# Feed-forward up projections: one 512-column matmul over both parts of the activations, and the closing steps moved to VectorE

## The reference, cut to what matters

```python
for i in range(4):
    ...
    h = modulate_2(rms_norm_2(x, norm_g[i, 2]), sh_f, sc_f)
    y = jnp.square(jax.nn.relu(h @ ffn_w1[i])) @ ffn_w2[i]
    x = x + g_f[:, None, :] * rms_norm_2(y, norm_g[i, 3])
```

## Time and profile before

| | us |
|---|---|
| median of 3 runs | 3532.57 |
| lowest and highest | 3532.52, 3533.49 |
| the profiled execution, its own time | 3530.79 |
| its span in the profile | 3528.8 |
| TensorE busy in the span | 2957.8 (84%) |
| VectorE busy | 1101.8 (31%) |
| ScalarE busy | 989.0 (28%) |

### The profile page before, as it was taken

The page is one execution under the profiler, slowest core; times in us unless marked ns, Lnnn a source line. Parts: engine busy times, 40 slices in busy tenths (PEclk is TensorE's granted clock), DMA queues, the critical chain, the costliest instruction groups (busy, mean ns, idle before and its releaser), DMA issues.

```text
span 3528.8 us, 40562 instructions
## 1 busy us (share of the span) xinstructions
PE 2957.8 (84%) x16176; PEld 1959.7 (56%) x16176; DVE 1101.8 (31%) x1997; ACT 989.0 (28%) x1818; POOL 55.1 (2%) x51
## 2 busy tenths in 40 slices
PE   5999787777789678787787997878998978988898
PEld 2343432222464342222356897666887867875797
DVE  1174200000131320000035444344436345433454
ACT  1211211110121210000034444334434444433443
POOL 0030000000000000000000000000000000000000
PEclk9999899999899789999988998769998999998899
DMA  9683089999512039999912664105664324751141
GB/s 402 258 352 160 25 361 428 428 428 428 230 72 76 0 123 428 429 428 428 428 51 96 252 276 189 48 21 212 268 262 152 144 96 176 293 204 72 49 180 70
DMA packets 59987, 796.13 MB, mean 226 GB/s; under 512 B 9114, under 2 KB 10029, under 8 KB 11501
## 3 DMA queue, kind: packets, MB, share of 16 engines
q1 hardware_dynamic: 54576, 788.03, 54.0%
q10 hardware_dynamic: 5309, 6.69, 0.6%
HBM read 793.64 MB, written 1.05 MB: 225 GB/s over the span
## 4 chain that ended last, share of the span: by engine, by line
PE 68%; DMA 18%; DVE 5%; ACT 5%; issue 2%; ACTq 1%; SPq 0%; DVEq 0%; POOL 0%; POOLq 0%
DMA ring<-in_t_up 15%; PE banks L1574 11%; PE banks L1564 10%; PE banks L733 8%; PE banks L872 8%; PE banks L1195 7%; PE banks L1069 4%; PE banks L639 3%; PE banks L854 2%; DMA ring<-in_t_down 2%; ACT arena L677 1%; PE banks L1169 1%; PE banks L1211 1%; PE banks L1226 1%; PE banks L1304 1%
## 5 line engine op out<-in xcount | busy, mean ns | idle before, releaser
L1195 PE MATMUL banks<-ring,arena 128*64 128x512 f32 x2048 | 479.3, 623 | 120.0 <-DMA ring<-in_t_up 66.9
L2434 DVE TENSOR_TENSOR ring_lo<-ring,w_hi 128x1024 fp32r<-128x1024 f32 x256 | 312.5, 1225 | 410.3 <-ACT w_hi L1904 410.3
L1195 PEld LDWEIGHTS banks<-ring,arena 128*64 128x64 f32 x2048 | 167.7, 143 | 429.8 <-issue 384.4
L1904 ACT CAST w_hi<-ring 128x1024 fp32r<-128x1024 f32 x256 | 266.8, 1047 | 450.2 <-PE banks L1574 225.4
L1564 PE MATMUL banks<-u_hi,w_hi 128*128 128x256 f32 x1024 | 296.4, 289 | 38.2 <-DVE ring_lo L2434 38.2
L1564 PE MATMUL banks<-u_lo,w_hi 128*128 128x256 f32 x1024 | 293.2, 286 | 0.0
L1564 PE MATMUL banks<-u_hi,ring_lo 128*128 128x256 f32 x1024 | 292.9, 286 | 0.0
L1574 PE MATMUL banks<-ffn_h_hi,w_hi 128*128 128x256 f32 x1024 | 292.9, 286 | 0.0
L733 PE MATMUL banks<-arena,ring 128*128 128x512 f32 (+1 forms) x768 | 271.8, 517 | 24.2 <-ACT arena L677 17.0
L1574 PE MATMUL banks<-ffn_h_lo,w_hi 128*128 128x256 f32 x1024 | 289.7, 283 | 0.0
L1574 PE MATMUL banks<-ffn_h_hi,ring_lo 128*128 128x256 f32 x1024 | 289.6, 283 | 0.0
(11 more groups left out here) (327 smaller groups left out, 4137.9 us busy)
## 6 DMA issues: line engine op xcount, KB each, us to landing
ring<-in_t_ada SPq DMA_DIRECT2D x72, 2048.0 KB, 14.8
ring<-in_t_gate SPq DMA_DIRECT2D x64, 2048.0 KB, 17.2
ring<-in_t_up SPq DMA_DIRECT2D x64, 2048.0 KB, 17.3
ring<-in_t_down SPq DMA_DIRECT2D x64, 2048.0 KB, 17.3
ring<-in_t_ffn SPq DMA_DIRECT2D x64, 2048.0 KB, 12.2
ring<-in_t_ret_in SPq DMA_DIRECT2D x12, 2048.0 KB, 8.7
ring<-in_t_in_cd SPq DMA_DIRECT2D x6, 2048.0 KB, 18.6
ring<-in_t_sb_in SPq DMA_DIRECT2D x6, 2048.0 KB, 13.1
```

Source lines behind the costliest of these rows:

```text
L1195: mm = nc.tensor.matmul(PS[64 * h:64 * h + 64, f.bank, :], x_cur[:, b, k, :], wview(un[h0 + h], KC)[:, k, :], start=(k == 0), stop=(k == K ...
L1904: nc.scalar.copy(w_hi[:, n % 4], w).then_inc(S("ffn_w_hi"), 1)
L2434: TT(w_lo, w, w_hi[:, n % 4].bitcast(F32), ALU.subtract).then_inc(S("ffn_w_lo"), 1)
```

## The change

Four edits:

1. `u_hi` and `u_lo` become views of one tile `u_pair`, in which the two parts of a chunk lie side by side, 2 x 256 columns.
2. An up quarter has two matmuls for each chunk in place of three: the high weights by all 512 columns (the high and the low activations) into the full bank, and the low weights by the 256 high columns into the bank's first half. The bank then holds two halves that have to be added.
3. ScalarE no longer touches the bank: its relu is gone.
4. VectorE, in place of the square, copies the second half of the bank to SBUF, adds the first half to it (this frees the bank), and computes max(h, 0) x h. Each of the three waits for the one before it.

```diff
-        u_hi, u_lo = (region_r(f"u_{part}", 12288 + 2048 * i, [KC, N]) for i, part in enumerate(("hi", "lo")))
+        u_pair = region_r("u_pair", 12288, [KC, 2, N])
+        u_hi, u_lo = u_pair[:, :, 0, :], u_pair[:, :, 1, :]
...
-                                for w, x in ((hi, u_hi), (hi, u_lo), (lo, u_hi)):
-                                    mm = nc.tensor.matmul(PS[:, f.bank, 0:N], w[:, q, :], x[:, q, :],
-                                                          start=(q == 0 and x is u_hi and w is hi),
-                                                          stop=(q == KC - 1 and w is lo))
+                                nc.tensor.matmul(PS[:, f.bank, :], hi[:, q, :],
+                                                 u_pair[:, q].rearrange("p s t -> p (s t)"),
+                                                 start=(q == 0), stop=False, skip_group_check=True)
+                                mm = nc.tensor.matmul(PS[:, f.bank, 0:N], lo[:, q, :], u_hi[:, q, :],
+                                                      start=False, stop=(q == KC - 1), skip_group_check=True)
...
-                        if 4 <= n < 12:
-                            f = plan[p + "up"][n - 4]
-                            f.full.wait(act, it)
-                            nc.scalar.activation(ffn_h[:, n // 4 - 1, n % 4, :], PS[:, f.bank, 0:N], ACT.Relu)\
-                                .then_inc(f.free.sem, 1)
...
-                            fu[n - 4].free.wait(dve, it)
-                            TT(h, h, h, ALU.mult).then_inc(S("ffn_squared"), 1)
+                            f = fu[n - 4]
+                            f.full.wait(dve, it)
+                            V_.tensor_copy(h, PS[:, f.bank, N:2 * N]).then_inc(S("ffn_low"), 1)
+                            dve.wait_ge(S("ffn_low"), 32 * i + n - 3 + it * 8)
+                            TT(h, PS[:, f.bank, 0:N], h, ALU.add).then_inc(f.free.sem, 1)
+                            f.free.wait(dve, it)
+                            STT(h, h, 0.0, h, ALU.max, ALU.mult).then_inc(S("ffn_squared"), 1)
```

## The result

The changed kernel takes 3551.05 us (median of 6 runs, 3547.51 to 3553.26), the kernel before 3532.23 us in the 6 runs beside them: a ratio of 1.0053, 95% interval 1.0040 to 1.0066. It is slower by 18.8 us; 3548.5 was forecast.

What follows compares the result with a forecast made beforehand. TensorE's pace was taken to bound the loops, so its waits are paid in full. Last layer +5.3 and other layers +10.6 gave +15.9 us on 3532.6: 3548.5 us, own range 3543 to 3554, whole range 3538 to 3563.

Steps and rivals of the forecast that it cites:

- the sum: Whole kernel: +5.3 us in the last layer and +10.6 us in the first three, together +15.9 us.
- TensorE's saving: Up quarters: merged matmuls shorten each from 2.88 to 2.77 us, saving 0.107, at most 13.7 us over 128 quarters.
- VectorE's prices: VectorE's new closing: copy, addition and max-and-multiply 0.42 us each; copy and addition advance the step by 0.45 each.
- The bank wait: Up quarters: TensorE waits 0.73 us for VectorE's addition before quarters 2, 4, 6 (last layer) or 2 alone (others).
- The transposes: After quarter 7, first three layers: the reduce ending VectorE's step 10 comes later, delaying them by 0.90 us an iteration.
- The costs set at nothing: Elsewhere: ScalarE's 128 dropped relus, weights' low parts, loads, SyncE's waits and the interleaved tile add nothing to the time.
- The waits stay covered: Up runs: neither bank nor transposes are later than today, -12.4 us, 3520 us; chance 6%.
- Only the transposes wait: Up runs: no wait for the bank, only one after quarter 7 in three layers; -1.6 us, 3531 us; chance 8%.
- VectorE as the bound: VectorE's step: a copy of 0.69 us makes it 2.98, over TensorE's 2.77; +30.5 us, 3563 us; chance 10%.
- A wide matmul that saves nothing: Up quarters: a wide matmul takes 0.240 us, quarters stay 2.88; +25.7 us, 3558 us; chance 5%.
- Its signs: Profile after: wide matmuls 0.227 us apart, even-quarter idles 0.6 to 0.8, transposes' idle 1.3 to 1.5, VectorE steps 2.7.

Runs made afterwards that it cites:

- Experiment 6: Each quarter's wide matmuls grouped before its narrow ones, in the changed kernel: 3552.7 us; also, with VectorE's work reordered, low weights over 512 columns too: 3619.5 us.
- Experiments 1 and 4: Changed kernel with four banks in the last layer: 3540.3 us; changed kernel with VectorE's copy, addition and square ahead of the weights' subtraction: 3524.23 us.
- experiment 3: Changed kernel with the modulation reduce moved to the start of VectorE's step 10, ahead of subtraction and closing: 3533.6 us in one execution.
- experiment 2: Changed kernel with the three old 256-column matmuls per chunk, keeping a three-instruction closing on VectorE: 3555.15 us, 1.0069 of before.
- `both_grouped`: Changed kernel with VectorE's closing, then reduce, ahead of the subtraction, and each quarter's wide matmuls before its narrow ones: 3515.77 us, 0.9954 of before.

## Why the prediction was right

Direction and place came out as forecast, and the size nearly: +15.9 us predicted, +18.8 measured, inside the forecast's own range of 3543 to 3554. Part of that closeness is luck. Where the change acts, in the up runs, the loss is 21.5 us, 5.6 more than the sum, nearly all of it from TensorE's saving; the rest of the program was 1.1 us shorter in the profile after, for no reason that the change gives. With the 21.5 alone the median would have been 3553.7, at the very end of the range. By its steps:

- **TensorE's saving.** Mis-sized, by half. A quarter went to 2.83 us, not 2.77, so it saves 0.053 and not 0.107: 6.8 us over 128 quarters in place of 13.7. The 0.2267 came from a stretch in which all matmuls have 512 columns; the new order alternates widths. Experiment 6 shows that it is the alternation. The other candidate beside the rows' 13 ns a chunk was 2.5 ns, by the rule of the Trainium skill, "TensorE: Matmul & The Clock Gate", section "Back-to-back issue gap"; the measured 7 lies between them. That section gives the rule for a matmul in isolation, and the prediction set it against a stream. For matmuls of one width on these operands the rows hold (0.120 and 0.227), which that rule puts at 0.109 and 0.216.
- **VectorE's prices.** Right: the copy 0.417, with no row of its own before, the addition 0.424, max-and-multiply 0.425; each dependent start 0.45 after the last.
- **The bank wait.** Right in place and count: the list of waits has 24 of TensorE for the addition, 12.4 us together, as 12 iterations with one and 4 with three make. TensorE is back at F + 3.45 with 0.07 of restart, 3.52 where 3.50 was forecast. Against the longer quarter the wait is 0.70, forecast 0.73. (The 0.47 in the brackets counts from a modelled end. From start to start it is 3436.22 - 3435.47 = 0.75 in place of 0.12, so 0.63, and the restart makes it 0.70.) That quarters 3, 5 and 7 don't wait and the modulation pieces cover 4 and 6 came out too. Experiments 1 and 4 take the wait away by two different means; in the last layer both leave up runs of 22.6, 8 x 2.83.
- **The transposes.** Right: from F + 3.41 to F + 4.33, forecast 4.31.
- **The sum, with the measured quarter.** Last layer: 3 x 0.70 - 8 x 0.053 = +1.68, measured 24.73 - 23.04 = 1.69. Other layers: 0.70 + 0.92 - 7 x 0.053 = +1.25, measured 1.20 to 1.35. Together 12 x 1.25 + 4 x 1.68 = +21.7, and +21.5 is what the up runs grew by.
- **The costs set at nothing.** ScalarE's 128 relus less changed nothing that can be seen, and no wait for a load or a weight's low part has come up in the up runs.
- **The rivals.** The waits stay covered: refuted by the 24 waits. Only the transposes wait: refuted by the same, and by experiment 3, in which the bank waits stay. VectorE as the bound: its premise, a copy of 0.69, is refuted by the 0.417. In the last layer of the changed kernel, step 9 follows step 8 without idle time, 2.73 us after it (2.71 forecast; the two rows below). That is the step's own length, and it is less than the quarter's 2.83. Before steps 6, 8 and 10 VectorE sits idle for 0.7 to 0.8 us, waiting for ScalarE's copy. So it keeps pace, with 0.10 to spare. Experiments 1 and 4 agree, but a small lag could have been hidden in both. A wide matmul that saves nothing: refuted by experiment 2, since the old matmuls are 0.3 us an up run slower than the wide ones. But the saving is only half of the forecast's.
- **Its signs.** The transposes' 1.35 us, VectorE's steps of 2.73 and the places of the waits are as announced. Two are not: the wide matmuls start 0.235 before their successor and not 0.227, and the idle times before the even quarters are 0.46 to 0.59 as the profile counts them, where 0.6 to 0.8 was announced, the wait from start to start.

The two rows on VectorE's pace, steps 8 and 9 of the last layer's third iteration:

```profile
3446.77 1.23 DVE L2431 TENSOR_TENSOR ring_lo<-ring,w_hi 128x1024 fp32r<-128x1024 f32 x1 [0.73 <-ACT w_hi L1906]
...
3449.50 1.22 DVE L2431 TENSOR_TENSOR ring_lo<-ring,w_hi 128x1024 fp32r<-128x1024 f32 x1
```

## What to carry to other kernels

Moving the read of a PSUM bank to another engine has to be judged by what stands in front of it in that engine's program order, not by the engine's busy share: VectorE was 31% busy over the span (56% around the last layer's loop), and the bank still came 1.8 us later than from ScalarE (F + 3.30 against F + 1.53). With two banks in turn, the release must come within one fill of the bank's end; the cure was the order of instructions, not fewer of them. When a chain of work leaves the bound engine for one reduce that belongs to something else, issue that reduce as early as its input allows: that alone was worth as much as the merged matmul.

## What the runs showed of the hardware

Matmuls of 256 columns with a weight load each start 0.120 us apart, and those of 512 columns 0.227; in alternation the pair takes 0.353, not 0.347. In groups of eight, the cost of the change sits in the first five wide matmuls after narrow ones, 0.228 to 0.236 each (`both_grouped`). Merging two 256-column matmuls that share their weights saves 13 ns where all matmuls are of one width (2 x 0.120 - 0.227) and 7 ns where widths alternate.
